# A decoder trunk: how many weight units begin with half of the tokens behind a normed phase

## Chip, cores and metric

One core of one Trainium2 chip. The metric is the device time of one execution in microseconds (us); the kernel before has 2141.93 us (median of 3 runs, 2141.06 to 2142.15).

## The reference

A decoder trunk of two layers, 256 tokens of width 2048, all in float32. Layer A mixes by a chunked gMLP, layer B by stick-breaking attention; each is followed by a gated MLP with a causal convolution of width 3 (inner width 5632). What matters here is what stands between two matrix products:

```python
h = h + rms_norm(mix, post_mix_g[layer])
f = conv_ffn(rms_norm(h, pre_ffn_g[layer]), ffn_w_up[layer], ...)
h = h + rms_norm(f, post_ffn_g[layer])
```

A product's output is normed, scaled and added to the stream h; h is normed again, and the next product multiplies it by its weights. The second layer also needs h, normed with another gain, for its keys and values.

## The kernel before

Every float32 product is made of rounded parts: a value is split into a high part (rounded to float32r) and a low part (the rest), and TensorE multiplies high by high, high by low and low by high. Weights arrive from memory in **units** of 256 rows by 512 columns (UK = 2 tiles of 128 rows). For each unit SyncE issues one load into `raw` (ring of 4), ScalarE casts it to `w_hi` (`units`, line 528, cast at 539), VectorE subtracts to get `w_lo` (`units`, line 882, at 887), and TensorE uses both. Semaphores tie them: `raw_loaded`, `unit_hi`, `unit_split`, `unit_used`. A load waits until the unit four before it is split (line 405), a cast until the unit four before it is used (line 538). Eight units make one block of 512 columns.

The work is a list of phases (lines 87 to 98). Some multiply the tokens' side by the weights and put tokens on partitions (`tokens_out`); their results are normed (`NORMED`: a_out, down0, b_out, down1). The others (`columns_out`) put columns on partitions and take the stream, transposed, from `x_parts`. Behind the first three normed phases follow up0, q_in and up1 (`BEHIND`). This text calls these three places **boundaries**.

At a boundary the stream is updated and transposed in **slots**, since PSUM has few banks free. A slot is two tiles of 128 columns of h. Slots 0 to 2 hold tokens 0 to 127 of tiles 0 to 5, slots 3 to 5 tokens 128 to 255 of the same tiles, slots 6 to 10 all tokens of tiles 6 to 15 (`EARLY` = 3, lines 305 to 310). TensorE transposes a slot into PSUM (`turn_slots`, 1515, at 1533), ScalarE writes its high part with a gain (`slot_high`, 588, at 593), VectorE its low part (`slot_low`, 1015, at 1021), and only then is the bank free for the slot that `SLOT_BEFORE` pairs with it. At q_in, each slot is also copied out of PSUM without the gain (`slot_keep`), the early ones by ScalarE (601), the late ones by VectorE (1011).

In `first_columns` (1379) TensorE begins the phase behind with units 0 to 2 and tokens 0 to 127 (`early_columns`, 1362; only products with `w_hi`, line 1371), then does the same units with tokens 128 to 255 and all products with `w_lo` (1374), then units 3 to 7 with all tokens (1407, 1410). The transposes stand between units in an order written out by hand. The second half of the tokens waits for a chain at the end of the normed phase: ScalarE squares the last block (561), VectorE makes the mean (`post_mean_of`, 930, at 932), GpSimd raises it to the power -1/2 (`rsqrt`, 438, at 440), VectorE updates the first 512 columns of tokens 128 to 255 in two pieces (`update_first`, 952, at 958) and the rest with `update_stream` (941, at 948); `gain_block` (913, at 918) takes the last result out of PSUM.

Each engine has its own hand-written order: `turn_and_split` of ScalarE (617) and of VectorE (968), `after_normed` (739 and 1187). GpSimd makes the low parts of units 1 and 2 (`unit_low`, 449, at 453). ScalarE also sums the squares of the new stream (`square_stream`, 564, at 577) for the next norm, whose factor TensorE spreads (`spread`, 1536) behind unit 7. The other block and all later ones run in `columns_out` (1421, at 1440 and 1443).

Of the kernel before, what the change touches and what calls it, by code (L numbers as in the profile page):

```python
# [39 lines left out]
RING = 4  # L40
# [25 lines left out]
def build_trunk(nc, x, pre_mix_g, post_mix_g, pre_ffn_g, post_ffn_g, a_w_in, a_v_norm_g, a_w_spatial,  # L66
# [9 lines left out]
    NB = D // BLK  # L76
# [6 lines left out]
    LAST = NB - 1  # L83
# [116 lines left out]
    with ExitStack() as ctx:  # L200
# [103 lines left out]

        EARLY = 3
        SPLIT_TILES = UK * EARLY
        SLOT_BANK = [4, 5, 6, 4, 5, 6, 7, 4, 5, 6, 7]
        SLOT_BEFORE = {3: 0, 4: 1, 5: 2, 7: 3, 8: 4, 9: 5, 10: 6}
        SLOTS = len(SLOT_BANK)
# [115 lines left out]
        def _(pool):  # L425
# [74 lines left out]
            for s, ph in enumerate(NORMED):  # L500
# [13 lines left out]
                for half in range(NH):  # L514
                    rsqrt(post_scale[:, half:half + 1], post_mean[:, half:half + 1], 1,
                          post_meaned, post_scaled, NH * s + half + 1)
                    if s + 1 < len(NORMED):
                        if half:

                            pool.wait_ge(h_new[1], NB * s + 2)  # L520
                        unit_low(BEHIND[s], half + 1)
                if s + 1 < len(NORMED):
                    pre_rsqrt(s + 1)
# [3 lines left out]
        def _(act):  # L527
# [89 lines left out]
            def turn_and_split(t, ph):  # L617
                slot_keep(t, (1,))
                units(ph.first, 2, 3)
                slot_high(t, (3, 4))  # L620
                slot_keep(t, (2,))
                units(ph.first, 3, RING)
                slot_keep(t, (3,))
                slot_high(t, (5, 6))
                slot_keep(t, (4,))
                units(ph.first, RING, RING + 1)
                slot_keep(t, (5,))
                slot_high(t, (7, 8))
                units(ph.first, RING + 1, RING + 2)
                square_stream(t, 0)  # L630
                slot_high(t, (9, 10))
                units(ph.first, RING + 2, RING + 3)
                square_stream(t, 1)
                units(ph.first, RING + 3, ph.units)
                square_stream(t, 2)
                square_stream(t, 3)
# [102 lines left out]
            def after_normed(s, nxt):  # L739

                square(s, LAST, (0,))
                units(nxt.first, 0, 2)
                slot_high(s + 1, (0, 1, 2))
                square(s, LAST, (1,))
                slot_keep(s + 1, (0,))
                turn_and_split(s + 1, nxt)
# [134 lines left out]
        def _(dve):  # L881
# [59 lines left out]
            def update_stream(s, c, half):  # L941

                dve.wait_ge(post_scaled, NH * s + half + 1)
                if half or c < LAST:
# [5 lines left out]
                                         op0=ALU.mult, op1=ALU.add).then_inc(h_new[half], 1)  # L950

            def update_first(s):

# [13 lines left out]

            def turn_and_split(t, ph):
                update_first(t - 1)
                update_stream(t - 1, 1, 1)  # L970
                slot_low(t, (3,))
                gain_block(t - 1, LAST, (1,))
                slot_low(t, (4,))
                update_stream(t - 1, 2, 0)
                update_stream(t - 1, 2, 1)
                slot_low(t, (5, 6))
                slot_keep(t, (6,))

                dve.wait_ge(unit_split, ph.first + EARLY)
                units(ph.first, 3, RING)  # L980
                update_stream(t - 1, 3, 0)
                update_stream(t - 1, 3, 1)
                slot_low(t, (7,))
                units(ph.first, RING, RING + 1)
                slot_low(t, (8,))
                slot_keep(t, (7, 8))
                units(ph.first, RING + 1, RING + 2)
                slot_low(t, (9,))
                units(ph.first, RING + 2, RING + 3)
                slot_low(t, (10,))  # L990
                units(ph.first, RING + 3, ph.units)
                slot_keep(t, (9, 10))
                pre_means(t)
# [193 lines left out]
            def after_normed(s, nxt):  # L1187
                begin_post_norm(s)
                post_norm(s, 0)
                update_stream(s, 0, 0)  # L1190
                units(nxt.first, 0, 1)
                update_stream(s, 1, 0)
                slot_low(s + 1, (0, 1, 2))
                post_mean_of(s, 1)
                turn_and_split(s + 1, nxt)
# [163 lines left out]
        def _(pe):  # L1359
# [19 lines left out]
            def first_columns(ph, t):  # L1379
# [3 lines left out]
                pe.wait_ge(evacuated, ph.block0 - 1)  # L1383
                for u in range(EARLY):
                    if u == EARLY - 1:
                        turn_slots(t, (3, 4))
                    pe.wait_ge(unit_hi, ph.first + u + 1)
                    early_columns(bank, u, x_parts, 0, t)
                for u in range(EARLY):
                    pe.wait_ge(unit_split, ph.first + u + 1)  # L1390
                    early_columns(bank, u, x_parts, 1, t)
                    if u == 0:
                        turn_slots(t, (5,))

                        pe.wait_ge(evacuated, ph.block0)
                        turn_slots(t, (6,))
                    if u == 1:
                        turn_slots(t, (7, 8))
                for u in range(EARLY, ph.units):
# [14 lines left out]
                    if u == EARLY:  # L1414
                        turn_slots(t, (9, 10))
                if t == KV_NORM:
# [318 lines left out]
```

## Time and profile before

| what | before |
|---|---|
| median of 3 runs | 2141.93 us |
| lowest, highest | 2141.06, 2142.15 us |
| the profiled execution | 2140.77 us |
| its span in the trace | 2139.0 us |
| TensorE matmuls busy | 2129.6 us |
| VectorE, ScalarE, GpSimd busy | 1432.1, 1014.8, 72.7 us |

The span is what the trace covers from the first to the last instruction; the execution's own time is 1.8 us longer. Busy time says how long an engine had an instruction in it; a matmul's record is longer than the distance to the next matmul, since they overlap, so distances between starts are read below, not durations. Rows of the timeline give the start in us, the duration, engine, line, what is written from what, and how many instructions are merged; behind them, in brackets, how long the engine had been idle and whose work ended that.

### The profile page before, as it was taken

How to read it: one execution, taken by the hardware profiler on the slowest of the kernel's cores; microseconds unless marked ns; L12 is line 12 of the kernel's file. 1: busy time of each engine (PE TensorE's matmuls, PEld its weight loads, DVE VectorE, ACT ScalarE, POOL GpSimd, SP SyncE). 2: the span in 40 equal slices, each digit the busy share in tenths (PEclk: the TensorE clock that was granted, in tenths of full speed). 3: DMA queues.
4: the chain of work that ended last, by engine and by line, in shares of the span. 5: the costliest groups of instructions: out<-in, count | busy, mean ns of one | idle time of the engine just before them, and what ended most of it. 6: DMA issues, size and time to landing. Idle time of an engine off the chain costs nothing.

```text
span 2139.0 us, 32149 instructions
## 1 busy us (share of the span) xinstructions
PE 2129.6 (100%) x11273; PEld 1826.9 (85%) x11273; DVE 1432.1 (67%) x1758; ACT 1014.8 (47%) x1174; POOL 72.7 (3%) x99
## 2 busy tenths in 40 slices
PE   9999999999999999999999999999999999999998
PEld 8888888888888888888888888888888888888887
DVE  5666577777877774444765675577878778774444
ACT  6445464444444444434644574464444444444433
POOL 0510010000000000000000010010000000000000
PEclk9999999999999999999999999999999999999999
DMA  7865656666666566665566544656666666666664
GB/s 258 231 207 176 198 175 190 187 184 196 188 193 187 177 218 199 193 193 180 187 189 189 177 154 154 204 175 189 189 180 198 189 193 187 180 221 192 193 195 149
DMA packets 210686, 407.31 MB, mean 190 GB/s; under 512 B 13488, under 2 KB 15920, under 8 KB 209968
## 3 DMA queue, kind: packets, MB, share of 16 engines
q1 hardware_dynamic: 207920, 398.51, 60.8%
q0 software_dynamic: 2640, 7.73, 1.1%
q8 instruction: 50, 0.82, 0.2%
q14 instruction: 28, 0.23, 0.0%
q10 hardware_dynamic: 48, 0.02, 0.0%
HBM read 404.10 MB, written 2.10 MB: 190 GB/s over the span
## 4 chain that ended last, share of the span: by engine, by line
PE 99%; issue 0%; ACT 0%; DVE 0%; DVEq 0%; POOLq 0%; POOL 0%; ACTq 0%
PE ps L1440 37%; PE ps L1443 18%; PE ps L1456 13%; PE ps L1454 13%; PE ps L1455 13%; PE ps L1407 1%; PE ps L1410 1%; PE ps L1371 1%; PE ps L1533 1%; PE ps L1374 0%; PE ps L1550 0%; PE ps L1612 0%; PE ps L1680 0%; PE ps L1651 0%; PE ps L1512 0%
## 5 line engine op out<-in xcount | busy, mean ns | idle before, releaser
L887 DVE TENSOR_TENSOR w_lo<-raw,w_hi 128x1024 fp32r<-128x1024 f32 x743 | 905.7, 1225 | 633.6 <-ACT w_hi L539 628.3
L539 ACT CAST w_hi<-raw 128x1024 fp32r<-128x1024 f32 x749 | 781.3, 1050 | 930.3 <-PE ps L1443 526.9
L1440 PE MATMUL ps<-x_parts,w_hi 128*128 128x512 f32 x3136 | 1089.3, 394 | 0.0
L1443 PE MATMUL ps<-x_parts,w_lo 128*128 128x256 f32 x3136 | 869.7, 277 | 0.0
L1440 PEld LDWEIGHTS ps<-x_parts,w_hi 128*128 128x128 f32 x3136 | 588.1, 188 | 137.2
L1443 PEld LDWEIGHTS ps<-x_parts,w_lo 128*128 128x128 f32 x3136 | 589.1, 188 | 0.0
L1454 PE MATMUL ps<-w_hi,g_parts 128*128 128x512 f32 x704 | 274.1, 389 | 0.0
L1456 PE MATMUL ps<-w_hi,g_parts 128*128 128x512 f32 x704 | 273.9, 389 | 0.0
L1455 PE MATMUL ps<-w_lo,g_parts 128*128 128x512 f32 x704 | 273.9, 389 | 0.0
L1455 PEld LDWEIGHTS ps<-w_lo,g_parts 128*128 128x128 f32 x704 | 132.1, 188 | 27.4
L1456 PEld LDWEIGHTS ps<-w_hi,g_parts 128*128 128x128 f32 x704 | 132.1, 188 | 27.4
L1454 PEld LDWEIGHTS ps<-w_hi,g_parts 128*128 128x128 f32 x704 | 132.1, 188 | 27.3
L1207 DVE SCALAR_TENSOR_TENSOR conv<-conv_in,conv_cols,conv 128x256 f32<-128x256 f32 x352 | 146.8, 479 | 0.0
L1440 PE MATMUL ps<-kv_parts,w_hi 128*128 128x512 f32 x256 | 88.8, 394 | 0.0
L757 ACT CAST g_parts<-conv 128x1024 f32 (+1 forms) x22 | 23.1, 1049 | 101.2 <-DVE conv L1231 101.2
L1443 PE MATMUL ps<-kv_parts,w_lo 128*128 128x256 f32 x256 | 70.9, 277 | 0.0
L1204 DVE TENSOR_SCALAR conv<-conv_in,conv_cols 128x256 f32<-128x256 f32 x176 | 60.7, 409 | 0.0
L1440 PEld LDWEIGHTS ps<-kv_parts,w_hi 128*128 128x128 f32 x256 | 48.0, 188 | 11.2
L910 DVE TENSOR_TENSOR conv_in<-conv_in,row_scale 128x1024 f32<-128x1024 f32 x44 | 54.0, 1226 | 1.5
L903 DVE TENSOR_TENSOR conv_in<-ps,low 128x1024 f32<-128x1024 f32 x44 | 53.6, 1218 | 0.0
L548 ACT COPY low<-ps 128x1024 f32<-128x1024 f32 x52 | 52.5, 1010 | 1.7 <-PE ps L1443 1.7
L1454 PE MATMUL ps<-w_hi,kv_parts 128*128 128x512 f32 x128 | 50.7, 396 | 0.0
(163 smaller groups left out, 1740.8 us busy)
## 6 DMA issues: line engine op xcount, KB each, us to landing
raw<-in_ffn_w_up SPq DMA_DIRECT2D x352, 512.0 KB, 3.7
raw<-in_ffn_w_down SPq DMA_DIRECT2D x176, 512.0 KB, 4.5
raw<-in_a_w_in SPq DMA_DIRECT2D x61, 512.0 KB, 4.6
raw<-in_a_w_out SPq DMA_DIRECT2D x32, 512.0 KB, 4.7
raw<-in_b_w_q SPq DMA_DIRECT2D x32, 512.0 KB, 4.5
raw<-in_w_k SPq DMA_DIRECT2D x32, 512.0 KB, 4.6
raw<-in_w_v SPq DMA_DIRECT2D x32, 512.0 KB, 4.7
raw<-in_b_w_o SPq DMA_DIRECT2D x32, 512.0 KB, 4.6
```

Of the source, the lines that this page charges most:

```text
L539: act.copy(w_hi[:, slot, :, :], raw[:, slot, :, :]).then_inc(unit_hi, 1)
L548: ins = act.copy(low[:, :, :], src) if scale is None else act.mul(low[:, :, :], src, scale)
L887: dve.tensor_tensor(w_lo[:, slot, :, :], raw[:, slot, :, :], w_hi[:, slot, :, :].bitcast(F32), ALU.subtract).then_inc(unit_split, 1)
L903: dve.tensor_tensor(to, src, low[:, :, :], ALU.add).then_inc(evacuated, 1)
L910: dve.tensor_tensor(to, to, row_scale[:, :].unsqueeze(1).to_broadcast([P, TB, T]), ALU.mult).then_inc(combined, 1)
L1204: ins = dve.tensor_scalar(conv[:, m, :], src, w, conv_cols[:, layer, TAPS, m, row], ALU.mult, ALU.add)
L1207: ins = dve.scalar_tensor_tensor(out=conv[:, m, :], in0=src, scalar=w, in1=conv[:, m, :], op0=ALU.mult, op1=ALU.add)
L1440: pe.matmul(ps[:, bank + m, :], w_hi[:, slot, kk, m * P:(m + 1) * P], src[:, kt, :, :].rearrange("p a t -> p (a t)"), start=first, stop=False,
L1443: mm = pe.matmul(ps[:, bank + m, 0:T], w_lo[:, slot, kk, m * P:(m + 1) * P], src[:, kt, HI, :], start=False, stop=last, skip_group_check=True)
L1454: pe.matmul(to, src[:, kt, HI, t0:t0 + P], w_hi[:, slot, kk, :], start=first, stop=False)
L1455: pe.matmul(to, src[:, kt, HI, t0:t0 + P], w_lo[:, slot, kk, :], start=False, stop=False)
L1456: mm = pe.matmul(to, src[:, kt, LO, t0:t0 + P], w_hi[:, slot, kk, :], start=False, stop=last)
```

## The change

`EARLY` becomes 4. So there are 12 slots: 0 to 3 with tokens 0 to 127 of tiles 0 to 7, 4 to 7 with tokens 128 to 255, 8 to 11 with all tokens of tiles 8 to 15. TensorE's order becomes: unit 0, slot 3, units 1 and 2, slots 4 and 5, unit 3 (all with tokens 0 to 127); unit 0, slots 6 and 7, unit 1, slots 8 and 9, units 2 and 3 (with tokens 128 to 255); unit 4, slots 10 and 11, units 5 to 7. Unit 2's high part is cast by VectorE (`third_high`, a new function) instead of ScalarE, and its low part made by VectorE instead of GpSimd. GpSimd makes unit 1's low part behind both powers, once the first update of tokens 128 to 255 is done. VectorE takes `gain_block` ahead of `update_first`, and slots 3 and 4 ahead of `update_stream(1, 1)`; it takes slots 10 and 11 ahead of the subtractions of units 6 and 7. ScalarE casts unit 3 before slot 3's high part (at q_in behind it), waits for the last `gain_block` before slot 3, and keeps slots 0 to 2 before all this at q_in.

```diff
-        EARLY = 3
+        EARLY = 4
-        SLOT_BANK = [4, 5, 6, 4, 5, 6, 7, 4, 5, 6, 7]
-        SLOT_BEFORE = {3: 0, 4: 1, 5: 2, 7: 3, 8: 4, 9: 5, 10: 6}
+        SLOT_BANK = [4, 5, 6, 4, 5, 6, 7, 4, 5, 6, 7, 4]
+        SLOT_BEFORE = {3: 0, 4: 1, 5: 2, 7: 3, 8: 4, 9: 5, 10: 6, 11: 7}
...
-                    if s + 1 < len(NORMED):
-                        if half:
-                            pool.wait_ge(h_new[1], NB * s + 2)
-                        unit_low(BEHIND[s], half + 1)
                 if s + 1 < len(NORMED):
+                    pool.wait_ge(h_new[1], NB * s + 1)
+                    unit_low(BEHIND[s], 1)
                     pre_rsqrt(s + 1)
...
             def turn_and_split(t, ph):
-                slot_keep(t, (1,))
-                units(ph.first, 2, 3)
-                slot_high(t, (3, 4))
-                slot_keep(t, (2,))
-                units(ph.first, 3, RING)
-                slot_keep(t, (3,))
-                slot_high(t, (5, 6))
-                slot_keep(t, (4,))
+                act.wait_ge(unit_hi, ph.first + 3)
+                if t != KV_NORM:
+                    units(ph.first, 3, RING)
+                act.wait_ge(evacuated, ph.block0)
+                slot_high(t, (3,))
+                if t == KV_NORM:
+                    units(ph.first, 3, RING)
+                slot_high(t, (4, 5))
+                slot_keep(t, (3, 4))
+                slot_high(t, (6, 7))
+                slot_keep(t, (5,))
                 units(ph.first, RING, RING + 1)
-                slot_keep(t, (5,))
-                slot_high(t, (7, 8))
+                slot_keep(t, (6,))
+                slot_high(t, (8, 9))
+                slot_keep(t, (7,))
+                square_stream(t, 0)
                 units(ph.first, RING + 1, RING + 2)
-                square_stream(t, 0)
-                slot_high(t, (9, 10))
+                slot_high(t, (10, 11))
                 units(ph.first, RING + 2, RING + 3)
...
-                slot_keep(s + 1, (0,))
+                slot_keep(s + 1, (0, 1, 2))
                 turn_and_split(s + 1, nxt)
...
+            def third_high(ph):
+                dve.wait_ge(raw_loaded[2], 16 * (ph.first // RING + 1))
+                dve.wait_ge(unit_used, ph.first + 2 - RING + 1)
+                dve.wait_ge(unit_hi, ph.first + 2)
+                dve.tensor_copy(w_hi[:, 2, :, :], raw[:, 2, :, :]).then_inc(unit_hi, 1)
...
             def turn_and_split(t, ph):
+                gain_block(t - 1, LAST, (1,))
                 update_first(t - 1)
+                slot_low(t, (3, 4))
                 update_stream(t - 1, 1, 1)
-                slot_low(t, (3,))
-                gain_block(t - 1, LAST, (1,))
-                slot_low(t, (4,))
+                slot_low(t, (5,))
+                dve.wait_ge(unit_split, ph.first + 2)
+                units(ph.first, 2, 3)
                 update_stream(t - 1, 2, 0)
                 update_stream(t - 1, 2, 1)
-                slot_low(t, (5, 6))
-                slot_keep(t, (6,))
-                dve.wait_ge(unit_split, ph.first + EARLY)
+                slot_low(t, (6, 7))
                 units(ph.first, 3, RING)
+                slot_low(t, (8, 9))
+                units(ph.first, RING, RING + 1)
                 update_stream(t - 1, 3, 0)
                 update_stream(t - 1, 3, 1)
-                slot_low(t, (7,))
-                units(ph.first, RING, RING + 1)
-                slot_low(t, (8,))
-                slot_keep(t, (7, 8))
+                slot_keep(t, (8, 9))
                 units(ph.first, RING + 1, RING + 2)
-                slot_low(t, (9,))
-                units(ph.first, RING + 2, RING + 3)
-                slot_low(t, (10,))
-                units(ph.first, RING + 3, ph.units)
-                slot_keep(t, (9, 10))
+                slot_low(t, (10, 11))
+                units(ph.first, RING + 2, ph.units)
+                slot_keep(t, (10, 11))
                 pre_means(t)
...
                 update_stream(s, 1, 0)
+                third_high(nxt)
                 slot_low(s + 1, (0, 1, 2))
...
                 for u in range(EARLY):
+                    if u == 1:
+                        turn_slots(t, (3,))
                     if u == EARLY - 1:
-                        turn_slots(t, (3, 4))
+                        turn_slots(t, (4, 5))
...
                     if u == 0:
-                        turn_slots(t, (5,))
                         pe.wait_ge(evacuated, ph.block0)
-                        turn_slots(t, (6,))
+                        turn_slots(t, (6, 7))
                     if u == 1:
-                        turn_slots(t, (7, 8))
+                        turn_slots(t, (8, 9))
...
                     if u == EARLY:
-                        turn_slots(t, (9, 10))
+                        turn_slots(t, (10, 11))
```

## Rows read from the trace of the kernel before

**Rows 1.** The page, part 4: the chain that ended last, shares of the span by engine.

```profile
PE 99%; issue 0%; ACT 0%; DVE 0%; DVEq 0%; POOLq 0%; POOL 0%; ACTq 0%
```

**Rows 2.** The list of waits, whole run: us in total, times, longest us.

```profile
PEld ps L1533 <- issue: 2.2, 6, 0.5
```

**Rows 3.** Timeline at the first boundary, TensorE: start, us, instruction [idle before].

```profile
282.33 2.07 PE L1371 MATMUL ps<-x_parts,w_hi 128*128 128x256 f32 x16
...
284.76 0.80 PE L1533 MATMUL ps<-ident,h 128*128 128x128 f32 x4 [0.37 <-DVE h L958]
...
285.32 1.40 PE L1371 MATMUL ps<-x_parts,w_hi 128*128 128x256 f32 x9
...
286.56 0.28 PE L1374 MATMUL ps<-x_parts,w_lo 128*128 128x256 f32 x1
...
288.23 0.29 PE L1374 MATMUL ps<-x_parts,w_lo 128*128 128x256 f32 x1
```

**Rows 4.** The same stretch, ScalarE, VectorE and GpSimd.

```profile
281.35 1.74 DVE L1021 SCALAR_TENSOR_TENSOR x_parts<-ps,gains,x_parts 128x128 fp32r<-128x128 f32 x6 [0.58 <-ACT x_parts L593]
...
283.12 1.04 ACT L539 CAST w_hi<-raw 128x1024 fp32r<-128x1024 f32 x1
...
283.54 0.55 POOL L440 TENSOR_TENSOR post_scale<-post_mean,half_neg 128x1 f32<-128x1 f32 x1 [0.50 <-DVE post_mean L932]
284.13 0.88 DVE L958 SCALAR_TENSOR_TENSOR h<-mixed,post_scale,h 128x256 f32<-128x256 f32 x2 [0.67 <-POOL post_scale L440]
...
285.21 1.14 ACT L593 ACTIVATE x_parts<-ps,gains 128x128 fp32r<-128x128 f32 x4 [1.06 <-PE ps L1533]
...
285.75 2.42 POOL L453 TENSOR_TENSOR w_lo<-raw,w_hi 128x1024 fp32r<-128x1024 f32 x1 [1.66 <-DVE h L948]
285.87 0.61 DVE L1021 SCALAR_TENSOR_TENSOR x_parts<-ps,gains,x_parts 128x128 fp32r<-128x128 f32 x2 [0.20 <-ACT x_parts L593]
...
287.51 1.87 DVE L948 SCALAR_TENSOR_TENSOR h<-mixed,post_scale,h 128x512 f32<-128x512 f32 x2
```

**Rows 5.** Timeline behind it, 291 to 305 us, all three engines.

```profile
292.09 1.41 DVE L948 SCALAR_TENSOR_TENSOR h<-mixed,post_scale,h 128x512 f32<-128x512 f32 x2
...
293.41 0.87 DVE L1021 SCALAR_TENSOR_TENSOR x_parts<-ps,gains,x_parts 128x256 fp32r<-128x256 f32 x2
...
293.71 0.40 PE L1407 MATMUL ps<-x_parts,w_hi 128*128 128x512 f32 x1
...
294.20 1.22 DVE L887 TENSOR_TENSOR w_lo<-raw,w_hi 128x1024 fp32r<-128x1024 f32 x1
...
295.33 0.87 DVE L1021 SCALAR_TENSOR_TENSOR x_parts<-ps,gains,x_parts 128x256 fp32r<-128x256 f32 x2
...
296.54 1.03 PE L1533 MATMUL ps<-ident,h 128*128 128x128 f32 x8
297.18 1.57 ACT L593 ACTIVATE x_parts<-ps,gains 128x256 fp32r<-128x256 f32 x4 [1.88 <-PE ps L1533]
...
298.62 1.07 ACT L539 CAST w_hi<-raw 128x1024 fp32r<-128x1024 f32 x1
...
299.72 1.23 DVE L887 TENSOR_TENSOR w_lo<-raw,w_hi 128x1024 fp32r<-128x1024 f32 x1 [0.79 <-ACT w_hi L539]
...
304.44 2.93 ACT L539 CAST w_hi<-raw 128x1024 fp32r<-128x1024 f32 x3
```

**Rows 6.** The chain that ended last, in order of time: start, us, what.

```profile
296.70 0.87 PE ps L1533 x8
```

**Rows 7.** Groups of instructions by line and shape, VectorE: count | busy us, mean ns.

```profile
L1048 DVE CAST w_hi<-raw 128x512 fp32r<-128x512 f32 x1 | 0.4, 427 | 0.8 <-DMA raw<-in_a_w_in 0.8
```

**Rows 8.** Timeline at the second boundary, 732.4 us later, ScalarE.

```profile
1015.51 0.64 ACT L601 COPY kv_raw<-ps 128x256 f32<-128x256 f32 x2
```

**Rows 9.** Windows of TensorE: us, busy (matmuls), granted clock, DMA share, GB/s.

```profile
98.00:180.00 82.00, 82.00 (x467) 1.00 0.65 198
330.00:770.00 440.00, 440.00 (x2540) 1.00 0.64 189
```

## The prediction

> **What bounds the kernel now.** The chain of work that ended last comes first: TensorE holds 99% of it [rows 1]. So only two things can move the time: TensorE's own instructions, and places where it waits. The list of waits gives the second: the transposes of line 1533 wait six times, up to 0.5 us each [rows 2], twice at each of three places. Three normed phases with a phase behind them (a_out, down0, b_out) give one such place each; I read the first in the timeline and use its clock below. The others repeat it, the second 732.4 us later.
>
> One early matmul costs 0.12 us: from 286.56 to 288.23 there are 14 steps, 1.67 / 14 [rows 3]. Sixteen from 282.33 would end at 284.25; the transposes start at 284.76, 0.51 late, because the stream's first half-block of tokens 128 to 255 is only written from 284.13 [rows 3, 4]. Four transposes at 0.11 (eight hold 0.87 of the chain [rows 6]) make 0.44, but the next matmul stands at 285.32: 0.12 more. Nine at 0.12 should bring 286.40 and the row says 286.56: 0.16 more, a wait for the low part of slot 3, the first with tokens 128 to 255. **TensorE loses 0.79 us at a boundary, 2.4 us in all, 0.11% of the run.** No version of this change can give back more than that.
>
> **The change, part by part.** (1) *Order on TensorE.* Before the wait now stand units 0, 1 and 2 with tokens 0 to 127 and two transposes: 282.33 + 24 x 0.12 + 2 x 0.11 = 285.43. The first piece of the half-block is ready near 284.6 (284.13 plus about half of the pair's 0.88 [rows 4]; so an end on VectorE reaches TensorE 0.15 later, at 284.76). The wait is covered with 0.8 us to spare: gain 0.79.
>
> (2) *The fourth early unit.* 24 matmuls x 0.12 = 2.88 in place of 8 pairs, which took 2.83 from 293.71 to 296.54 [rows 5]: +0.05. Unit 4 now follows an early unit directly, as unit 3 did, and should take that pace of 0.353 a pair instead of the 0.347 of a long stretch (440 us / 1270 pairs [rows 9]): +0.05. Together +0.10.
>
> (3) *Slot 4.* Before, from the first transpose (284.76) ScalarE began its high part at +0.45 (285.21), VectorE the low part at +1.11 (285.87), and TensorE's first matmul with tokens 128 to 255 stood at 286.44 (one step ahead of 286.56), +1.68 [rows 3, 4]. Now between transpose and that matmul lie 4 transposes and 8 matmuls, 0.44 + 0.96 = 1.40. Waits of 0.28, and 0.05 for the second tile: +0.33. Second halves begin at 287.1.
>
> (4) *VectorE casts unit 2* (third_high), between the update and slot_low of slots 0 to 2. It has no row of its size; the nearest is its cast of 128x512 at 0.43 us [rows 7]. I take twice that, 0.85, as the same operation on twice the columns; bounds are 0.43 below and 1.22 above, a subtraction of 128x1024 [rows 5]. From 280.7 it ends about 281.5, when the low parts could begin at 281.35 anyway [rows 4]; TensorE needs the first at 282.33. Cover: that slack of 0.6 us; cost 0. At 1.22 the cover breaks: +0.18 at the first tiles, and some 0.15 further on. In exchange ScalarE loses the cast at 283.12 and puts unit 3 there, before slot 3's high parts; those are wanted by TensorE only at 285.87, so nothing waits. gain_block ahead of the first update takes 0.6 us in the gap that VectorE spends on GpSimd's power at 283.54 [rows 4]: cost 0.
>
> (5) *GpSimd* gives unit 2's low part to VectorE (+1.13 of its time) and takes unit 1's after the first update: 285.1 + 2.42 = 287.5 [rows 4], wanted by TensorE at 289.5. SP's queue: the load of unit 5 waits for this split and starts late, at 287.6, but ScalarE comes to cast it only near 295, behind slot 9 and a square. Cost 0.
>
> (6) *VectorE's queue up to unit 4.* It stands idle until slot 4 is transposed (285.43 + 1.11 = 286.55). Then: slot 4, 0.6; update 0.66; slot 5, 0.6; subtraction of unit 2, 1.13; two updates 1.32; slots 6 and 7, 1.16; unit 3, 1.13; slots 8 and 9, 1.58; unit 4, 1.22 [rows 4, 5]. Sum 9.4: 295.95, and 0.15 to TensorE, 296.1. TensorE gets there at 287.1 + 64 x 0.12 + 12 x 0.11 = 296.1 too. The two meet; a stall can only add, so I take 0.1, with bounds 0 and 0.4.
>
> (7) *Unit 6, the new wait.* The last transposes now follow unit 4, not unit 3: they start at T = 296.2 + 2.83 = 299.05, and behind them lies one unit less before unit 6. ScalarE's cast of unit 6 is queued behind slot_high of the last two slots. The old rows give the chain: T = 296.54; high parts 297.18 (T + 0.64); cast 298.62 (T + 2.08); subtraction 299.72 (T + 3.18), 1.23 long, and 0.15 to TensorE: T + 4.56 [rows 5]. TensorE wants unit 6 at T + 0.87 + 2.78 = T + 3.65. Before, another unit of 2.78 lay between and hid it with 1.9 us. **Now TensorE waits 0.9 us.** That VectorE takes both slots' low parts ahead of this subtraction costs nothing extra: they end before the cast does.
>
> (8) *Unit 8.* ScalarE's cast of it stood at 304.44, T + 7.90 [rows 5], splits at T + 10.2; TensorE arrives at T + 10.3. Stall 0 to 0.2, I take 0.03.
>
> (9) *q_in's boundary* also keeps slots. Slot 3's transposes follow kept slot 0, which ScalarE copies only behind the last square: 283.11 + 0.39, and 0.15 to TensorE, 283.65 against 283.29 [rows 8] (the pair of copies stands at 283.11 on this clock, and the first ends some 0.39 later). +0.36, of which some 0.06 comes back at unit 4: +0.3, once.
>
> Sum at a boundary: -0.79 + 0.10 + 0.33 + 0.10 + 0.90 + 0.03 = +0.67; three times +2.0, and 0.3: **+2.3 us**. The profiled execution took 2140.77 (span 2139.0), 1.2 below the median 2141.93; its durations are used for a difference only, so I forecast 2141.93 + 2.3 = **2144.2**. This is within 0.2% (4.3 us), which is about what a measurement of this kernel can tell from no change.
>
> **Rivals.** *The gain holds* (15%): unit 6 does not wait, since something in the chain of T + 4.56 is shorter than in the old order. For it: VectorE was idle 0.79 us before that subtraction, so the chain is ScalarE's alone [rows 5]. Against: every link of it is still there in the new program text. Then -0.79 + 0.10 and up to 0.46 of (3), (6): -0.7 to -0.2 a boundary, 2140 to 2141.5.
>
> *VectorE becomes the bound* (12%): place, unit 4's subtraction; the two meet there. Any 0.1 us that VectorE's queue is later from 286.55 on is 0.1 us of the run, three times. Price: cast at 1.22, +0.3; update beside GpSimd. Two updates from 287.51 took 1.87 instead of 1.41 while GpSimd ran until 288.17 [rows 4, 5], 0.46 more; the new update(1,1), wanted at 287.15, falls beside GpSimd's instruction to 287.5: up to 0.35. Together 0.65 a boundary: 2144.2 + 2.0 = 2146.2, at the edge of what counts as slower, and above it with unit 8's 0.2. The Trainium skill (SBUF — State Buffer, Who interferes with whom) says that a VectorE instruction with two SBUF inputs and a GpSimd one exclude each other for a whole instruction. By that rule alone the update would start at 287.5, (6) would be 0.4 and the time 2145.1. The old row agrees in kind, but delays 0.46 where the rule has 0.66 (288.17 - 287.51).
>
> *The pace breaks, slower* (4%): pairs of lines 1440 and 1443 ran at 82 us / 233.5 = 0.351 through one phase and at 0.3465 through another, at the same granted clock of 1.00 [rows 9]; behind an early unit 0.353, behind transposes the fast one [rows 5]. If the restart after the new wait at unit 6 or 8 left TensorE in the slow pace for the phases behind (3136 pairs), it would be 14 to 20 us: 2158 to 2164. It decides at unit 8; two transposes stand right before it, behind which the old trace is always fast, hence 4%.
>
> *The change doesn't do what it says*: I find each order in the diff; nothing for it, inside the 1% left.
>
> **How the numbers follow.** The likeliest case (68%) has 2144.2, own range 2142.5 to 2145.5. Of the rest, 15% lies at 2140 to 2141.5, 12% around 2146. The range 2140.4 to 2146.8 leaves out the pace, part of the 12% and the lowest of the gain. Slower by over 0.2% (above 2146.2): half of VectorE's case, the pace, 11% with a little of the main case. Faster by over 0.2% (below 2137.6) needs more than the whole 2.4 us of waits: 2%. Within: 87%.
>
> **What would show it.** In the changed kernel: no idle at the first transposes of line 1533 behind 24 matmuls; a wait of about 0.3 us before the first matmul with tokens 128 to 255 on ScalarE or VectorE's x_parts; one of about 0.9 us before unit 6 for w_lo, some 21.3 us after the boundary's start; 0.36 us before slot 3 at q_in alone; pairs at 0.3467 behind that. No wait at unit 6 makes the forecast wrong downwards, w_lo waits over 0.4 us at unit 4 or a pace of 0.353 upwards.

## The result, and the profile after

The changed kernel took 2151.89 us (median of 15 executions) against 2141.06 (median of 15 beside it, where the forecast started from 2141.93 of 3): the ratio is 1.0049, 95% interval [1.0036, 1.0062]. The forecast was 2144.2, range 2140.4 to 2146.8; both the time and the call "within 0.2%" were wrong. The median is not the whole result, though. The executions, sorted:

```
before  2140.32 ... 2142.15 (15 executions, all within 1.8)
after   2142.30 2142.32 2142.37 2143.03 2143.20
        2151.31 2151.51 2151.89 2152.13 2152.20 2154.28
        2160.47 2160.98 2161.02 2164.09
```

There are levels, about 9 us apart, and single executions 3 us above the second and the third. The lowest level is 1.2 to 2.1 us above the kernel before, where the sum had +2.3; the rest is something else.

The page of the changed kernel, first part, and its waits of TensorE (total us, times, longest):

```profile
PE 2142.1 (100%) x11297; PEld 1837.3 (85%) x11297; DVE 1436.6 (67%) x1769; ACT 1015.0 (47%) x1179; POOL 64.4 (3%) x96
```

```profile
PE ps L1417 <- DVE w_lo L891: 1.9, 3, 0.6
PE ps L1522 <- DVE ones_r L1042: 1.1, 1, 1.1
```

The waits of line 1533 (now 1543) for the stream's update are gone [rows 2]; in their place stands one at each boundary for `w_lo`, at the first matmul of unit 6. In the timeline of the first boundary (start, duration, instruction):

```profile
280.46 0.69 DVE L961 CAST w_hi<-raw 128x1024 fp32r<-128x1024 f32 x1
...
283.17 2.15 PE L1380 MATMUL ps<-x_parts,w_hi 128*128 128x256 f32 x16
...
284.84 2.39 POOL L453 TENSOR_TENSOR w_lo<-raw,w_hi 128x1024 fp32r<-128x1024 f32 x1 [1.00 <-DVE h L969]
...
285.16 0.60 PE L1543 MATMUL ps<-ident,h 128*128 128x128 f32 x4
...
285.51 1.57 PE L1380 MATMUL ps<-x_parts,w_hi 128*128 128x256 f32 x9
...
286.76 1.01 DVE L952 SCALAR_TENSOR_TENSOR h<-mixed,post_scale,h 128x512 f32<-128x512 f32 x1
```

Four transposes at 285.16 follow the 24 early matmuls without a wait, where those at 284.76 stood 0.51 late [rows 3]. Further on, all three engines:

```profile
298.62 1.04 PE L1543 MATMUL ps<-ident,h 128*128 128x128 f32 x8
```

```profile
299.25 1.57 ACT L591 ACTIVATE x_parts<-ps,gains 128x256 fp32r<-128x256 f32 x4 [3.82 <-PE ps L1543]
...
300.12 1.66 DVE L1029 SCALAR_TENSOR_TENSOR x_parts<-ps,gains,x_parts 128x256 fp32r<-128x256 f32 x4 [2.04 <-ACT x_parts L591]
...
300.69 1.07 ACT L537 CAST w_hi<-raw 128x1024 fp32r<-128x1024 f32 x1
...
301.79 1.23 DVE L891 TENSOR_TENSOR w_lo<-raw,w_hi 128x1024 fp32r<-128x1024 f32 x1
...
303.07 0.50 PE L1417 MATMUL ps<-x_parts,w_hi 128*128 128x512 f32 x1 [0.64 <-DVE w_lo L891]
```

This is the chain foreseen for unit 6: transposes at T = 298.62, high parts at T + 0.63, cast at T + 2.07, subtraction at T + 3.17, TensorE at T + 4.45. The old one had T + 0.64, 2.08 and 3.18 [rows 5].

Where the 13.5 us of the profiled execution (2154.28 us; span 2152.6 against 2139.0) really lie is seen only in the long phases that the change does not touch. Their matmuls come in **pairs**, one of 512 columns with `w_hi` and one of 256 with `w_lo` (lines 1450 and 1453). Windows of TensorE in up0, in q_in and k_in, and in up1 (us, busy, matmuls, granted clock, DMA share, GB/s):

```profile
330.00:770.00 440.00, 440.00 (x2492) 1.00 0.63 186
1060.00:1190.00 130.00, 130.00 (x738) 1.00 0.60 190
1450.00:1870.00 420.00, 420.00 (x2425) 1.00 0.64 190
```

In up0 440 us held 2492 matmuls instead of 2540 [rows 9], at the same granted clock of 1.00: a pair takes 440 / 1246 = 0.353 us instead of 0.3465. In q_in and k_in it is 130 / 369 = 0.352. In up1 it is 420 / 1212.5 = 0.346, as before. up0 has 1344 pairs behind the boundary's first block, up1 as many, q_in and k_in 448. At 0.0067 us a pair that is 9.0, 9.0 and 3.0 us. So the levels can be read: 2142.3 none slow, 2151.5 one up phase, 2160.5 both, 3 more where q_in and k_in are slow too. The profiled execution has up0 and q_in/k_in: 2142.3 + 9.0 + 3.0 = 2154.3, and 2154.28 was measured. By their levels, 5 of the 15 executions had no slow up phase, 6 one, 4 both; only the profiled one has a trace.

The trace also shows where the slow pace began. Around unit 8 at the first boundary:

```profile
306.29 0.40 PE L1417 MATMUL ps<-x_parts,w_hi 128*128 128x512 f32 x1
...
308.37 0.40 PE L1417 MATMUL ps<-x_parts,w_hi 128*128 128x512 f32 x1
...
308.73 0.38 PE L1549 MATMUL ps<-ident,pre_scale 128*128 128x128 f32 x2
308.87 0.50 PE L1450 MATMUL ps<-x_parts,w_hi 128*128 128x512 f32 x1
309.20 0.28 PE L1453 MATMUL ps<-x_parts,w_lo 128*128 128x256 f32 x1
```

Six pairs of units 6 and 7 take 308.37 - 306.29 = 2.08 us, 0.347 each: the pace behind the 0.6 us wait at unit 6 is fast, and so it is at the other two boundaries. The slow pairs start behind unit 8's first matmul. The packed trace gives starts to the ns: to the second matmul of unit 8 it is 335, 335 and 333 ns at the three boundaries, against 313 in the kernel before. TensorE waited there for 0.02 to 0.03 us each time; behind it up0 and q_in/k_in were slow, up1 was fast.

**The theories then.** The rival with 4%, a broken pace, had happened. What remained was why. Below, a **tie** is a place where VectorE ends a unit's low part just when TensorE wants it, so that TensorE waits some ten ns or not at all. *Theory 1*: TensorE waits behind the boundary, and the way in which it starts again leaves a phase in one of two paces for good. The changed kernel offers two places: the 0.7 us at unit 6, and unit 8, where VectorE's subtraction ended at 307.59 + 1.22 = 308.81 and TensorE asked at 308.84. *Theory 2*: the four early units or the new order as such do it.

### The profile page after: what moved, and what is told of

Its sections match the earlier page's. It is cut to its first block, busy times and chain, and to the rows that moved or that the text cites. A ratio compares the mean times of both kernels' runs of the same rounds, so it can differ in the third digit from the quotient of the medians.

```text
span 2152.6 us, 32216 instructions
## 1 busy us (share of the span) xinstructions
PE 2142.1 (100%) x11297; PEld 1837.3 (85%) x11297; DVE 1436.6 (67%) x1769; ACT 1015.0 (47%) x1179; POOL 64.4 (3%) x96
## 4 chain that ended last, share of the span: by engine, by line
PE 99%; DVE 0%; issue 0%; ACT 0%; DVEq 0%; POOLq 0%; POOL 0%; ACTq 0%
PE ps L1450 37%; PE ps L1453 19%; PE ps L1466 13%; PE ps L1465 13%; PE ps L1464 13%; PE ps L1380 1%; PE ps L1417 1%; PE ps L1383 1%; PE ps L1543 0%; PE ps L1420 0%; PE ps L1560 0%; PE ps L1622 0%; PE ps L1690 0%; PE ps L1661 0%; DVE x_parts L1029 0%
## 5 line engine op out<-in xcount | busy, mean ns | idle before, releaser
L1453 PE MATMUL ps<-x_parts,w_lo 128*128 128x256 f32 x3136 | 879.6, 280 | 0.0
```

The costliest lines, as they stand in the source:

```text
L1453: mm = pe.matmul(ps[:, bank + m, 0:T], w_lo[:, slot, kk, m * P:(m + 1) * P], src[:, kt, HI, :], start=False, stop=last, skip_group_check=True)
```

## The experiments

Each stands beside the kernel before, whose median was between 2140.96 and 2141.10 us each time, its executions between 2140.4 and 2142.3. No experiment leaves out a part of the computation; the memsets write a buffer that is free there.

**1. Two spare transposes ahead of the spread (e1).**

```diff
             def spread(t):
                 pe.wait_ge(pre_scaled, t + 1)
+                for _ in range(2 if t else 0):
+                    pe.transpose(ps[:, row_bank(t), 0:P], ident[:, :], ident[:, :])
```

> Changed kernel with two spare transposes ahead of the two that spread the norm's factor behind unit 7, at all three boundaries, so that TensorE asks for unit 8 some 0.22 us later. In the changed kernel's trace it asked within 0.03 us of the end of VectorE's subtraction. Theory 1 (the near tie at unit 8 leaves TensorE in the slow pace in part of the executions): no wait at unit 8, all executions in one level at 2142.3 + 0.7 = 2143.0 us. Theory 2 (the 0.7 us wait at unit 6 does it, and unit 8 has nothing to do with it): the executions still scatter over 2143, 2152, 2161 and 2164 us.

Measured: 2164.4, 2164.7, 2165.0 and 2165.1 us, one level, but the highest: all phases slow, always. Ratio 1.0111 [1.0096, 1.0126]. Windows:

```profile
330.00:770.00 440.00, 440.00 (x2492) 1.00 0.63 185
1060.00:1190.00 130.00, 130.00 (x738) 1.00 0.62 189
1450.00:1870.00 420.00, 420.00 (x2379) 1.00 0.63 186
```

Both forms of theory fail as stated: with no wait at unit 8 the pace was not fast, and the time did not scatter. In this trace the pairs of unit 6 were at 0.353 already, right behind the wait, and stayed there through four transposes. So the pace need not be made anew at unit 8: here it was carried over the transposes, while in the changed kernel's own trace it turned slow at unit 8. Why these four transposes always ended slow is not settled.

**2. ScalarE's cast of unit 6 first (e2).**

```diff
-                units(ph.first, RING + 1, RING + 2)
+                units(ph.first, RING + 1, RING + 3)
                 slot_high(t, (10, 11))
-                units(ph.first, RING + 2, RING + 3)
```

> Changed kernel with ScalarE's cast of unit 6 ahead of the high parts of slots 10 and 11. That takes the wait at unit 6 away (0.69 us at each boundary in the trace) and lets ScalarE reach unit 8's cast about 0.9 us earlier in relation to slots 10 and 11, so unit 8 has 0.2 us to spare. Theories 1 and 2 both expect one level, near 2142.3 - 3 x 0.7 = 2140.2 us. A third theory (four early units as such upset the pace) expects the scatter to stay, at levels 2 us lower.

Measured: 2142.3 to 2164.2 over 11 executions, median 2154.22, ratio 1.0055 [1.0035, 1.0075]. The scatter stayed, but the edit had not done its work: TensorE still waited 0.5 us at unit 6, now for VectorE, which takes the low parts of slots 10 and 11 ahead of unit 6's subtraction. The prediction had called that order free, since ScalarE's cast was the later of the two; with the cast out of the way it is the next to bind. At unit 8 nothing waited in this trace, and yet up1 was slow; its pairs were slow from unit 6 on. At the other two boundaries the same wait at unit 6 was followed by fast pairs.

**3. A late unit 8 (e3).**

```diff
                 pre_means(t)
+                dve.memset(conv[:, :, :], 0.0)
```

> Changed kernel with a VectorE memset of 128x1024 (0.91 us) behind the means, so that unit 8's subtraction ends some 0.3 us after TensorE asks for it, at each boundary. Theory 1 in its narrow form (only a wait of some ten ns upsets the pace): one level, 2142.3 + 1.0 = 2143.3 us. Theory 1 in its wide form (any wait at unit 8): all executions at 2164 us or nearly. Theory 2: the scatter stays as it is, from 2143 to 2165 us.

Measured: 2152.6, 2161.2, 2162.2, 2164.5, 2165.1; ratio 1.0105 [1.0091, 1.012]. At unit 8 TensorE waited 0.25 us at each boundary. In the profiled execution the pairs were slow ahead of that wait at all three boundaries; behind it two phases ran fast and one slow. So a wait does not lock the slow pace; it can end it too.

**4. and 10. The phase gate_u (e4, e10).** By the starts of its matmuls it runs at 0.353 us a pair in every trace of the other runs, the kernel before's too. e4 puts two transposes ahead of it, e10 one:

```diff
             pe.wait_ge(row_ready, 1)
+            for _ in range(2):
+                pe.transpose(ps[:, 4, 0:P], ident[:, :], ident[:, :])
             with pe.Fori(0, gate_u.pairs) as i:
```

> Kernel before with two spare transposes of the identity ahead of the phase gate_u, which ran at 0.353 us a pair (256 pairs) right behind another kind of matmul. If the way in which a phase is entered sets the pace of all of it, gate_u runs at 0.347 and the time falls by 256 x 0.0066 - 0.22 = 1.5 us, to 2139.6 us. If the pace belongs to the phase's data or banks, the time rises by 0.2 us.

> Kernel before with one spare transpose ahead of gate_u, where two left its pace at 0.353. If the pace of a phase is set by the place in a cycle of three steps at which it is entered, one step less may give 0.347: 2141.1 - 1.7 + 0.1 = 2139.5 us. If it is always slow when it comes from the normal stream: 2141.2 us.

Measured: 2141.52 us, ratio 1.0002 [0.9993, 1.0011], and 2140.80, ratio 0.9999 [0.999, 1.0008]. gate_u's pairs stayed at 0.353 in both, but for the first. A cost as small as two transposes' 0.2 us is inside the intervals; at this place one or two transposes do not make the pace fast.

**5. No wait at units 6 and 8 (e5).**

```diff
                 square_stream(t, 0)
-                units(ph.first, RING + 1, RING + 2)
+                units(ph.first, RING + 1, RING + 3)
+                square_stream(t, 1)
                 slot_high(t, (10, 11))
-                units(ph.first, RING + 2, RING + 3)
-                square_stream(t, 1)
...
-                units(ph.first, RING + 1, RING + 2)
+                units(ph.first, RING + 1, RING + 3)
                 slot_low(t, (10, 11))
-                units(ph.first, RING + 2, ph.units)
+                units(ph.first, RING + 3, ph.units)
```

> Changed kernel with three moves: on ScalarE and on VectorE unit 6 ahead of slots 10 and 11, and ScalarE's second square of the stream ahead of their high parts. By the walk unit 6 is split before the transposes begin and unit 8 some 1.2 us before TensorE asks for it, so there is no wait at unit 6 (0.69 us in the changed kernel) and none at unit 8. Theory 1 (a wait of TensorE that is followed by whole units leaves the pace of all that follows open, fast or slow, and where there is none the pace behind the last transposes is fast): one level, 2142.3 - 3 x 0.7 = 2140.2 us. Theory 2 (four early units or the new order upset the pace by themselves): the executions still scatter over some 20 us.

Measured: six executions at 2139.35 to 2140.42, six at 2148.2 to 2150.3; ratio 1.0013 [1.0001, 1.0026]. The lowest level is where it was expected, the two-up-phase level is gone, but one phase was still slow in half of the executions. The list of waits names none at the boundaries. Only the starts show what is left. Unit 4's first pair and the next, in this trace:

```profile
295.95 0.41 PE L1416 MATMUL ps<-x_parts,w_hi 128*128 128x512 f32 x1
296.20 0.28 PE L1419 MATMUL ps<-x_parts,w_lo 128*128 128x256 f32 x1
296.32 0.40 PE L1416 MATMUL ps<-x_parts,w_hi 128*128 128x512 f32 x1
```

From the first to the second matmul it is 0.25 us. In the kernel before, at its first whole unit, it is 0.23:

```profile
293.71 0.40 PE L1407 MATMUL ps<-x_parts,w_hi 128*128 128x512 f32 x1
293.94 0.28 PE L1410 MATMUL ps<-x_parts,w_lo 128*128 128x256 f32 x1
294.06 0.40 PE L1407 MATMUL ps<-x_parts,w_hi 128*128 128x512 f32 x1
```

VectorE's subtraction of unit 4 started at 294.60 and took 1.21, to 295.81; TensorE asked for its weights at about 295.83. The two met within some ten ns, at the place where the prediction had them meet. To the ns, the first two matmuls of unit 4 are 246, 233 and 244 apart at the three boundaries: two ties and one entry without. Of the phases behind the two ties up0 was slow and up1 fast. Units 5 to 7 ran at 0.347 at the first boundary too; its slow pairs begin behind the spread, without a wait there. That the tie is to blame rests on run e9 below.

**6. and 14. The wait at unit 6 kept, unit 8 freed (e6, and e14 with unit 4 freed too, by e12's edit below).**

```diff
                 units(ph.first, RING + 1, RING + 2)
+                square_stream(t, 1)
                 slot_high(t, (10, 11))
                 units(ph.first, RING + 2, RING + 3)
-                square_stream(t, 1)
```

> Changed kernel with ScalarE's second square of the stream alone ahead of slots 10 and 11: unit 8 then has 1.2 us to spare, but the 0.7 us wait at unit 6 stays. If the wait at unit 6 alone can leave the pace slow, the executions still scatter over 2142, 2151 and 2161 us. If only the tie at unit 8 does it, one level at 2142.3 us.

> Changed kernel with e6's and e12's moves together: no tie at unit 4, 1.2 us to spare at unit 8, the 0.7 us wait at unit 6 kept. Theory 1 (any wait): scatter from 2142 up, with slow phases. If the wait at unit 6 is harmless because the two transposes behind unit 7 set the pace anew: one level near 2142.3 us.

Measured: e6 has 5 executions at 2142.5 to 2143.7 and 7 at 2151.2 to 2152.8, ratio 1.0036 [1.0024, 1.0047]; e14 one at 2142.9, five at 2151.6 to 2152.4, one at 2161.5 and one at 2163.9, ratio 1.0059 [1.0039, 1.0079]. In e14 the wait at unit 6 is the only one left behind the first units: it is enough. Its trace has slow pairs in units 6 and 7 at all three boundaries; behind the two transposes of the spread two phases became fast and one stayed slow.

**7. The kernel before with a wait at unit 6 (e7).**

```diff
                 slot_low(t, (9,))
+                for _ in range(3):
+                    link(dve.memset(conv[:, :, :], 0.0))
                 units(ph.first, RING + 2, RING + 3)
```

> Kernel before with three linked memsets of 128x1024 on VectorE (some 0.95 us each) ahead of unit 6's subtraction: TensorE then waits some 0.4 us at unit 6 at each boundary, and nothing else of the change is there. Theory 1: the executions scatter from 2142 up to 2164 us. Theory 2: one level, 2141.1 + 1.2 = 2142.3 us.

Measured: 2156.6, 2162.8, 2162.9, 2163.0, ratio 1.0101 [1.0087, 1.0116]; the waits were 0.6, 1.6 and 0.6 us. They account for some 3 us; the rest is the pace. Nothing of the change is in this kernel, so the new order is not needed for the slow pace; e9 shows that it is not enough either.

**8. The kernel before with a wait at unit 8 (e8).**

```diff
                 pre_means(t)
+                for _ in range(3):
+                    link(dve.memset(conv[:, :, :], 0.0))
```

> Kernel before with three linked memsets of 128x1024 on VectorE behind the means: TensorE waits some 0.5 us at unit 8, behind the two transposes that spread the factor. Theory 1: scatter from 2142.6 up to 2164 us. Theory 2: one level, 2141.1 + 1.5 = 2142.6 us.

Measured: 2164.6, 2164.7, 2165.2, 2165.2, ratio 1.0111 [1.0096, 1.0126]. One place, one wait of about 1 us a boundary, and 23.8 us more, of which some 3 are the waits:

```profile
308.28 0.38 PE L1541 MATMUL ps<-ident,pre_scale 128*128 128x128 f32 x2
309.48 0.50 PE L1442 MATMUL ps<-x_parts,w_hi 128*128 128x512 f32 x1 [0.82 <-DVE w_lo L887]
```

```profile
330.00:770.00 440.00, 440.00 (x2493) 1.00 0.63 185
1060.00:1190.00 130.00, 130.00 (x737) 1.00 0.61 190
1450.00:1870.00 420.00, 420.00 (x2379) 1.00 0.63 186
```

Up to the spread the trace is the kernel before's, fast pairs included. Behind the wait all three are slow.

**9. No tie at unit 4 either (e9).** e5, and on VectorE:

```diff
-                slot_low(t, (8, 9))
+                slot_low(t, (8,))
                 units(ph.first, RING, RING + 1)
+                slot_low(t, (9,))
```

> The kernel without waits at units 6 and 8 (e5) with one more move: VectorE makes unit 4's low part ahead of slot 9's, so that it ends some 0.9 us before TensorE asks for it; in e5 the two met within some ns (the first pair of unit 4 took 0.246 us to its second matmul where the kernel before has 0.234), and one phase was slow in half of the executions. Theory 1, widened (any wait of TensorE, be it of some ns, among or right before whole units leaves the pace open): one level between 2139.3 and 2140.4 us. Theory 2 (four early units or the new order as such): half of the executions still near 2149 us.

Measured: 11 executions from 2139.33 to 2140.22, median 2139.92, one level; ratio 0.9994 [0.9985, 1.0003]. The slowest of them is faster than the fastest of the 29 of the kernel before beside them (2140.48 to 2142.22); the 95% interval still holds 1, so the gain itself is not shown beyond it. The forecast's terms without the wait at unit 6 and without the ties, with the sizes measured below, are three times (-0.79 + 0.10 + 0.26) and 0.3, -1.0 us; the medians differ by 2139.92 - 2140.96 = -1.04. e5 and e9 differ only in the tie at unit 4: with it 6 of 12 executions had a slow phase, without it none of 11. Unit 4 is entered as in the kernel before, with 0.23 us to the second matmul, and the long phases run fast:

```profile
296.44 0.40 PE L1417 MATMUL ps<-x_parts,w_hi 128*128 128x512 f32 x1
296.67 0.28 PE L1420 MATMUL ps<-x_parts,w_lo 128*128 128x256 f32 x1
296.79 0.40 PE L1417 MATMUL ps<-x_parts,w_hi 128*128 128x512 f32 x1
```

```profile
330.00:770.00 440.00, 440.00 (x2540) 1.00 0.63 189
1060.00:1190.00 130.00, 130.00 (x752) 1.00 0.62 190
1450.00:1870.00 420.00, 420.00 (x2425) 1.00 0.63 188
```

**11. and 13. A tie at unit 8 in the kernel before (e11, e13).** As e8, with shorter memsets: in e11 two of 1024 columns; in e13

```diff
                 pre_means(t)
+                link(dve.memset(conv[:, :, :], 0.0))
+                link(dve.memset(conv[:, :, 0:231], 0.0))
+                link(dve.memset(conv[:, 0, 0:32 * (2 * t - 1)], 0.0))
```

> Kernel before with two linked memsets behind the means in place of e8's three: VectorE ends unit 8's subtraction within 0.1 us of TensorE's asking, as in the changed kernel. Theory 1: executions scatter between 2141.2 and 2163 us, as the changed kernel's. If only a clear wait (1 us in e8: all phases slow) upsets the pace: one level, 2141.2 us.

> Kernel before with three linked memsets behind the means (1024 and 924 columns, and 32, 96 or 160 by boundary), some 0.28, 0.33 and 0.38 us more than e11's, which ended unit 8's subtraction 0.25 us before TensorE asked. TensorE now meets it within 0.1 us at each boundary. If a tie is enough to leave the pace open: executions scatter between 2141 and 2163 us. If only a long wait is: one level near 2141.3 us.

e11 missed: the subtraction ended 0.19 us ahead of unit 8's first matmul, where that distance is 0.055 to 0.059 us in every trace in which TensorE waits; nothing waited, and the 11 executions stood at 2140.5 to 2142.3. It shows that two memsets there do no harm by themselves. e13 hit at two of its three boundaries. One execution stood at 2140.9, nine at 2143.6 to 2144.5 and one at 2152.7: by the levels, q_in and k_in slow nearly always, an up phase once; ratio 1.0011 [1.0003, 1.002]. In its profiled execution the three boundaries differ by design. At the second, the spread's transposes and unit 8:

```profile
1040.73 0.38 PE L1542 MATMUL ps<-ident,pre_scale 128*128 128x128 f32 x2
1040.86 0.49 PE L1443 MATMUL ps<-x_parts,w_hi 128*128 128x512 f32 x1
1041.19 0.28 PE L1446 MATMUL ps<-x_parts,w_lo 128*128 128x256 f32 x1
1041.31 0.40 PE L1443 MATMUL ps<-x_parts,w_hi 128*128 128x512 f32 x1
...
1041.66 0.40 PE L1443 MATMUL ps<-x_parts,w_hi 128*128 128x512 f32 x1
...
1042.02 0.40 PE L1443 MATMUL ps<-x_parts,w_hi 128*128 128x512 f32 x1
...
1042.37 0.40 PE L1443 MATMUL ps<-x_parts,w_hi 128*128 128x512 f32 x1
```

and at the third:

```profile
1428.97 0.38 PE L1542 MATMUL ps<-ident,pre_scale 128*128 128x128 f32 x2
1429.15 0.50 PE L1443 MATMUL ps<-x_parts,w_hi 128*128 128x512 f32 x1
1429.49 0.28 PE L1446 MATMUL ps<-x_parts,w_lo 128*128 128x256 f32 x1
```

The first boundary has no wait and 0.31 us from unit 8's first matmul to the second, as the kernel before. At the second it is 0.33, by the packed trace 329 ns against 313: a wait of some 16 ns. The three pairs behind it take 1042.37 - 1041.31 = 1.06 us, the slow pace from the start. At the third the matmul itself comes 0.05 us later. Behind them:

```profile
330.00:770.00 440.00, 440.00 (x2541) 1.00 0.64 189
1060.00:1190.00 130.00, 130.00 (x738) 1.00 0.61 186
1450.00:1870.00 420.00, 420.00 (x2379) 1.00 0.62 186
```

2541 matmuls are fast; 738 and 2379 are slow. **The 448 pairs behind a wait of 16 ns ran slow, and so did the 1344 behind one of 0.05 us; those behind the boundary without a wait did not.** That is one execution. The nine at 2143.6 to 2144.5 have q_in and k_in slow alone, so there the third boundary mostly left up1 fast: a wait of this size opens the pace, it does not fix it.

**12. The tie at unit 4 alone removed (e12).**

The kernel is the changed one with e9's move on VectorE alone.

> Changed kernel with only the move of e9 on VectorE (unit 4's low part ahead of slot 9's); the waits at unit 6 (0.7 us) and the tie at unit 8 stay. Theory 1: still scattered, 2142 to 2164 us, since units 6 and 8 still wait. If the tie at unit 4 is what matters: one level at 2142.2 us.

Measured: 2142.9, 2143.2, 2145.7, 2151.9, 2153.1, 2155.0; ratio 1.004 [1.0024, 1.0056]. Still scattered, as theory 1 has it: freeing unit 4 alone is not enough. In its trace unit 8 did not wait; the pairs of units 6 and 7 were slow there, TensorE came later, and the tie had opened by itself. All three long phases were fast.

## Why the prediction was wrong

By its steps, at the first boundary (its parts in brackets):

- **The wait for the first update, (1).** Right: gone, -0.79.
- **Slot 4, (3).** +0.33 forecast, 0.26 measured (0.19 ahead of the first matmul with tokens 128 to 255, 0.07 between it and the next).
- **VectorE's cast, (4).** 0.85 taken, 0.69 measured (the row at 280.46 above), within the bounds, hidden as said. The row at 286.76 above shows the update beside GpSimd's subtraction (284.84 to 287.23): 1.01 us instead of the usual 0.74, 0.27 more. The Trainium skill (SBUF — State Buffer, Who interferes with whom) has whoever issues first hold the shared ports for the whole instruction; an estimate by that rule is a delay to GpSimd's end, 287.23 - 286.76 = 0.47. The trace agrees in direction, and it is 0.20 short of the estimate, as the old row is (0.46 against 0.66).
- **VectorE's queue, (6).** The two met at unit 4, as computed. 0.1 forecast; 0 to 0.015 measured by the first two matmuls of unit 4 (239, 233 and 248 ns apart at the three boundaries, where an entry without a wait has 233).
- **Unit 6, (7).** 0.9 forecast; 0.90 measured: the matmul ahead of the wait starts at 302.15, so the next would stand at 302.27 and stands at 303.07, 0.80 late, and the one behind it 0.10 more. (The list of waits counts only the 0.6 of the first, the expectations 0.7.)
- **Unit 8, (8).** 0.03 forecast, 0.03 measured.
- **q_in's slot 3, (9).** 0.36 forecast, 0.32 measured.

The terms of the sum thus held but for that 0.1, and with them the lowest level: 2142.3 to 2143.2 against a forecast of 2144.2, which started from a median of 3 executions, 0.9 above that of the 15. With the measured sizes in place, three times (-0.79 + 0.10 + 0.26 + 0.90 + 0.03) and 0.3 give +1.8, inside the 1.2 to 2.1 us by which the lowest level stands above the kernel before.

**The step that failed is the price of a stop of TensorE among whole units.** Parts (6) and (8) found that VectorE and TensorE would meet at units 4 and 8 and priced this at 0.1 and 0.03 us, part (7) priced the wait at unit 6 at 0.9: each time the length of the wait alone. The runs show that each of the three places leaves the pace of the phases behind it open, at 9.0 us for a slow up phase and 3.0 for q_in and k_in: unit 4 by e5 against e9, unit 6 by e14, unit 8 by e8 and e13. Some ten ns are enough, and how often the slow pace follows differs from place to place. The rival "the pace breaks" had the mechanism, the place (unit 8) and a fair price (14 to 20 us for all phases; 21 measured, and the 0.351 behind its lower bound is 0.353 by the starts of gate_u's matmuls), but got 4%, with the reason that "two transposes stand right before it, behind which the old trace is always fast". That read a coincidence as a cause. In the old trace nothing waits among the whole units and the pairs are fast already as they come to the transposes; e8 has the same two transposes and a wait behind them and was slow in all phases, e14 has no wait behind them and one phase was slow. In hindsight, with a wait of 0.9 us forecast at each of three boundaries and ties at two more units, the levels above 2150 deserved far more than 4%, and the range should have reached 2164. *The gain holds* and *VectorE becomes the bound* did not come; the latter's decision point, unit 4, was real, but by way of the pace.

What stays open: what makes the two paces, why the changed kernel's stops end fast in part of the executions and e8's never, and why e1's four transposes end slow each time.

## What to carry to other kernels

When TensorE is busy for 99% of the span, compare its rate in stretches that the change doesn't touch (matmuls in a window) ahead of looking for waits: here 0.6 us of listed wait at a boundary, or a tie that no list names, came with up to 9 us behind it. Give the engines that feed TensorE a margin at the start of each long stream instead of a tie, and treat a forecast tie as a risk for the whole phase behind it. And time such a kernel in ten executions or more: a single one of the changed kernel could have shown 2142 or 2164.

## What the runs showed of the hardware that was not expected

A stream of alternating matmuls of 512 and 256 columns, all with one granted clock of 1.00, has two stable paces, 0.3465 and 0.353 us a pair, and each persisted through loops and changes of block: the fast one for 477 us of up0 in the kernel before, the slow one for 475 us in e8. The starts, to the ns, show a rhythm. The slow pace repeats every three pairs (350, 361 and 349 ns, 1060 together), gate_u's too; the fast one every two (343 and 350), or it stands at 347. In the changed kernel's up0 a pair takes 353.3 ns both while VectorE is busy all through it and while it is idle, so VectorE's work is not what slows it. The pace can change where TensorE waits, if only for 16 ns (e13), and can change over transposes without a wait. There, the place in the rhythm went with the outcome: in the traces of e2, e6, e7, e12 and e14 slow pairs reach the spread's two transposes and unit 8 does not wait at 11 boundaries; in the 8 where unit 7's first two matmuls were 240 or 241 ns apart the phase behind was fast, in the 3 with 232 to 236 it was slow. No run was made to test this. Waits that are followed by narrow matmuls and several groups of transposes did no harm: the kernel before has them at each boundary [rows 2] and stayed within 2 us each time. VectorE's float32 cast of 128x1024 took 0.69 us, little more than half of the 1.22 of a subtraction of that size.
